# One kernel, three reorderings: a new opening, a first stage that projects one tile ahead, and a convolution stage with its gate products two tiles ahead

## The reference, cut to what matters

```python
h = rmsnorm(x, n1) * (1 + sc1) + sh1
u = h @ w_in                      # 1024 -> 7168 columns, split into branches
u_hy, u_fn, u_rx, u_ry, u_g = jnp.split(u, SPLITS, axis=-1)
kf  = hyena_filters(L, fw1, fb1, fw2, fb2, fw3, ffreq)   # two small sin layers, rfft
y_a = hyena_branch(u_hy, hcw, hcb, kf, hbias) @ w_a      # short conv, 2 long convs by FFT
y_b = fnet_branch(u_fn) @ w_b
xr  = depthwise_conv(u_rx, rcw, rcb, 2, 1)
h_f, s_f = rglru_scan(xr, ..., reverse=False); h_b, s_b = rglru_scan(xr, ..., reverse=True)
y_c = ((h_f + h_b) * gelu(u_ry)) @ w_c
ga, gb, gc = jnp.split(jax.nn.sigmoid(u_g), 3, axis=-1)
x = x + g1 * ((ga * y_a + gb * y_b + gc * y_c) @ w_o)    # then norm, SwiGLU FFN
```

## Time and profile before

| | before |
|---|---|
| median of three runs | 2571.53 us (2570.34 to 2575.14) |
| profiled execution | 2571.76 us, its span 2569.9 us |
| TensorE busy | 2479.5 us, 96% |
| DVE, ACT, GpSimd busy | 1460.8, 620.9, 696.0 us |
| mean granted clock of TensorE | 0.983 |
| DMA | 234.26 MB, mean 91 GB/s |

### The profile page before, as it was taken

The page is one execution under the profiler, slowest core; times in us unless marked ns, Lnnn a source line. Parts: engine busy times, 40 slices in busy tenths (PEclk is TensorE's granted clock), DMA queues, the critical chain, the costliest instruction groups (busy, mean ns, idle before and its releaser), DMA issues. The chain is left out here.

```text
span 2569.9 us, 34710 instructions
## 1 busy us (share of the span) xinstructions
PE 2479.5 (96%) x13478; PEld 2102.7 (82%) x13478; DVE 1460.8 (57%) x2697; ACT 620.9 (24%) x889; POOL 696.0 (27%) x300
## 2 busy tenths in 40 slices
PE   5799999999997999999999999999999999999997
PEld 2588888877876888888878878888888888888886
DVE  5878786678777676777763474633223322333236
ACT  4422222575753222222210012300000000000004
POOL 1011111223121222222333460442314331342220
PEclk8799999999998999999999999999999999999999
DMA  7244443111232222222453250111101010110002
GB/s 303 84 162 157 161 157 135 65 55 51 82 122 104 101 100 100 100 100 107 155 212 126 88 193 20 50 49 34 34 31 49 33 49 16 49 49 33 25 25 83
DMA packets 53755, 234.26 MB, mean 91 GB/s; under 512 B 6131, under 2 KB 8755, under 8 KB 48068
## 3 DMA queue, kind: packets, MB, share of 16 engines
q1 hardware_dynamic: 53700, 233.54, 25.2%
HBM read 178.98 MB, written 54.53 MB: 91 GB/s over the span
## 5 line engine op out<-in xcount | busy, mean ns | idle before, releaser
L840 PE MATMUL ps<-h_hi,w_hi 128*128 128x512 f32 (+1 forms) x2112 | 762.1, 361 | 13.5 <-DVE h_lo L1799 6.3
L841 PE MATMUL ps<-h_lo,w_hi 128*128 128x512 f32 (+1 forms) x2112 | 751.0, 356 | 0.0
L842 PE MATMUL ps<-h_hi,w_lo 128*128 128x512 f32 (+1 forms) x2112 | 750.9, 356 | 0.0
L798 POOL TENSOR_TENSOR w_hi<-w_raw,zero_col 128x1024 fp32r<-128x1024 f32 x96 | 206.4, 2150 | 1583.9 <-PE ps L842 1385.4
L840 PEld LDWEIGHTS ps<-h_hi,w_hi 128*128 128x128 f32 x2112 | 401.3, 190 | 78.8 <-issue 14.6
L842 PEld LDWEIGHTS ps<-h_hi,w_lo 128*128 128x128 f32 x2112 | 401.1, 190 | 57.1
L841 PEld LDWEIGHTS ps<-h_lo,w_hi 128*128 128x128 f32 x2112 | 401.5, 190 | 56.4 <-issue 0.2
L2151 DVE TENSOR_TENSOR a<-sil,ps 128x512 f32<-128x512 f32 (+1 forms) x66 | 39.5, 599 | 504.1 <-PE ps L842 501.7
L801 POOL TENSOR_TENSOR w_lo<-w_raw,w_hi 128x1024 fp32r<-128x1024 f32 x96 | 270.1, 2813 | 7.5
L2174 DVE SCALAR_TENSOR_TENSOR x<-ps,mod,x 128x512 f32<-128x512 f32 (+1 forms) x264 | 172.3, 661 | 98.1 <-PE ps L842 97.6
L841 PE MATMUL ps<-h_lo,wf_hi 128*128 128x512 f32 (+1 forms) x624 | 224.4, 360 | 0.0
(11 more groups left out here) (277 smaller groups left out, 3506.2 us busy)
## 6 DMA issues: line engine op xcount, KB each, us to landing
w_raw<-in_weights SPq DMA_DIRECT2D x146, 512.0 KB, 3.5
ada_w<-in_w_ada SPq DMA_DIRECT2D x18, 1024.0 KB, 8.1
scratch_gate_s<-g_st SPq DMA_DIRECT2D x24, 640.0 KB, 3.3
side<-scratch_gate_s SPq DMA_DIRECT2D x24, 640.0 KB, 4.0
scratch_k_s<-kstage SPq DMA_DIRECT2D x8, 1536.0 KB, 6.6
hy_k<-scratch_k_s SPq DMA_DIRECT2D x8, 1536.0 KB, 8.5
scratch_hy_s<-hout SPq DMA_DIRECT2D x16, 640.0 KB, 3.2
ada_early<-in_w_ada SPq DMA_DIRECT2D x6, 1024.0 KB, 22.2
```

The lines of the kernel that those rows point to most:

```text
L798: nc.gpsimd.tensor_tensor(hi[:], w_raw[slot % 2][:], zero_col[:].to_broadcast([P, D]), ALU.add).then_inc(pool_step, 1)
L840: mm(out, w_pair[0], x_pair[0], start=first, stop=False)
L841: mm(out, w_pair[0], x_pair[1], start=False, stop=False)
L842: return mm(out, w_pair[1], x_pair[0], start=False, stop=last)
```

## The change

**Opening.** The times of the filter network are laid out as two halves of 768, one in partitions 0 to 63 and one in 64 to 127 (`HALF_TILES`; the tiles 8 and 9 stand in both). `filter_layer` does each piece for both halves in separate quadrants of TensorE. ACT and DVE take 768 columns on 128 partitions in place of 1280. The squares come first, all of them summed before the first angle; the squares' product stands ahead of the second layer, the row product 0 before the broadcast of `rstd`. The four modulation rows have a row tile each; their turns go into one bank, and DVE adds the bias of all four in one instruction behind the scaling of x. `softplus` is moved behind the first stage.

**First stage.** Tile 1 is projected before the loop, and pass i holds tiles 2i+2 and 2i+3 where it held 2i+1 and 2i+2. The last pass holds tile 16, which belongs to the second stage, and the zeroing of the edges of `rin`. The first pair of the second stage is written out without tile 16, on TensorE and ACT. `load_ahead` of SyncE and its stores of `hout` are shifted in the same way.

**Convolution.** The first half is: tile t; transposes; tile t+1; tile t+2, piece 0; and goes on as the others. The others are: tile t, piece 2; tile t+1, pieces 0 and 1; transposes; tile t+1, piece 2; tile t+2, piece 0; forward transforms; tile t+2, piece 1; inverse singles and 2 pairs; tile t+2, piece 2; last 2 pairs; tile t+3, pieces 0 and 1, which the last half leaves out. ACT's gates and copies follow the same order, with tile t+2, piece 0 ahead of the `hy_z` copies. `store_gate` on SyncE, for the first gate of a half, stands ahead of the wait for `z_ready` and the loads. The store of the last scan and the states moves into the first half, behind its first gate store. The first channel block is written out; the loops run over the rest.

The core of the diff:

```diff
+HALF_TILES = ((0, 1, 4, 5, 8, 9), (2, 3, 6, 7, 8, 9))
+HALF_T = 6 * P
...
+            def filter_layer(layer, w_at, rows_at):
+
+                for j, (a, e) in enumerate(HALF_PIECES):
+                    out, done = mix_unit(u_setup, 0, FILT_UNIT[2 * layer + j])
+                    for half in range(2):
+                        rows = slice(half * FILT_HID, (half + 1) * FILT_HID)
+                        ins = mm(out[rows, 0:e - a], w_at(rows), rows_at(half, rows, a, e), start=True, stop=True)
+                    ins.then_inc(done, 1)
+
+            def row_product(r):
+                ada_row_unit(u_setup, 0, ROW_UNIT[r], [2 * r, 2 * r + 1], 16)
+
+            def row_turn(r):
+
+                if r == 0:
+                    mix_unit(u_setup, 0, TURN_UNIT)
+                pe.wait_ge(ada_row_ready, r + 1)
+                b = u_setup.bank(TURN_UNIT)
+                for q in range(4):
+                    ins = mm(mix(b)[:, 8 * r + 2 * q:8 * r + 2 * q + 2], ada_rows[r][:, q * P:(q + 1) * P],
+                             vec[:, V_SEL:V_SEL + 2], start=True, stop=True)
+                if r == ROWS_FIRST - 1:
+                    ins.then_inc(mix_done[b], 1)
...
             pe.wait_ge(consts_set, 3)
+            out, done = mix_unit(u_setup, 0, SQUARES_UNIT)
+            pe.wait_ge(x_sq_summed, KD - 1)
...
+            filter_layer(1, lambda rows: f_w2[rows, :], lambda half, rows, a, e: h1f[rows, a:e])
+
             pe.wait_ge(csilu_set, 2)
+            row_product(0)
+
+            pe.wait_ge(diag_ready, 1)
+            for b, (a, e, _) in enumerate(PIECES):
...
+            row_product(1)
+            row_product(2)
             pe.wait_ge(vec_in, 16)
...
+            row_turn(0)
+            row_turn(1)
+            row_product(3)
+            row_turn(2)
+            row_turn(3)
...
-                projection_tile(2 * i + 1, 1)
+                projection_tile(2 * i + 2, 0)
...
-                    projection_tile(2 * i + 2, 0)
+                    projection_tile(2 * i + 3, 1)
 
             projection_tile(0, 0, h_ready)
             taps_units(u_taps, 0, 0, 16)
+            projection_tile(1, 1)
...
+            def store_gate(c, j):
+                for b in range(3):
+                    sp.wait_ge(proj_free[b], 6 * c + (L3_TILE0 + j + 2))
+                sp.dma_start(dr["gate_s"][6 * c + j], g_st[:]).then_inc(gate_stored, 16)
...
                     load_ahead(t + 3 * order, 3 * order % 2)
-
+                    store_gate(c, 3 * order)
+                    if first and order == 0:
+                        sp.wait_ge(zc_ready, KD + 1)
+                        sp.wait_ge(zc_stored, 16 * KD + 16)
+                        sp.dma_start(dr["zc_s"][KD - 1], g_ry[1][:]).then_inc(zc_stored, 16)
+                        sp.dma_start(dr["state_out"], fin[:]).then_inc(fin_stored, 16)
+                        sp.wait_ge(zc_stored, 16 * (2 + KD))
                     sp.wait_ge(z_ready, 2 * c + (order + 1))
...
+            def l3_half(c, order, first, last):
...
+                if first:
+                    projection_tile(t, slot)
+                else:
+                    projection_tile(t, slot, pieces=(2,))
+                    projection_tile(t + 1, 1 - slot, pieces=(0, 1))
...
+                projection_tile(t + 1, 1 - slot, pieces=(0, 1, 2) if first else (2,))
+                projection_tile(t + 2, slot, pieces=(0,))
+
+                pe.wait_ge(hya_ready, 4 * c + (2 * order + 1))
...
+                projection_tile(t + 2, slot, pieces=(1,))
+
+                pe.wait_ge(y_ready, 4 * c + (2 * order + 1))
...
+                    if j == 2:
+                        projection_tile(t + 2, slot, pieces=(2,))
+                        pe.wait_ge(y_ready, 4 * c + (2 * order + 2))
...
+                if not last:
+                    projection_tile(t + 3, 1 - slot, pieces=(0, 1))
...
-                    gate(0)
+                    if first and order == 0:
+                        gate(0)
+                    else:
+                        gate(0, (2,))
+                        gate(1, (0, 1))
...
-                    gate(1, (0, 1))
+                    gate(1, (0, 1, 2) if first and order == 0 else (2,))
+                    gate(2, (0,))
```

More of the change, by code:

```diff
@@ L890, in _ @@
             pe.wait_ge(filt1_in, 32)
-            for j, (a, e, _) in enumerate(PIECES):
-                out, done = mix_unit(u_setup, 0, FILT_UNIT[j])
-                mm(out[0:FILT_HID, 0:e - a], f_w1[:, :], feats[:, a:e], start=True, stop=True).then_inc(done, 1)
+            filter_layer(0, lambda rows: f_w1[:, :], lambda half, rows, a, e: feats[:, half * HALF_T + a:half * HALF_T + e])
             pe.wait_ge(consts_set, 3)
+            out, done = mix_unit(u_setup, 0, SQUARES_UNIT)
+            pe.wait_ge(x_sq_summed, KD - 1)
@@ L896, in _ @@
+            for tile in range(NT):
+                ins = mm(out[:, 2 * tile:2 * tile + 2], x_sq_sum[:, tile * P:(tile + 1) * P], ones[:, 0:2],
+                         start=True, stop=True)
+            ins.then_inc(done, 1)
             pe.wait_ge(filt_in, 32)
             pe.wait_ge(sin_ready, 1)
-            for j, (a, e, _) in enumerate(PIECES):
-                out, done = mix_unit(u_setup, 0, FILT_UNIT[3 + j])
-                mm(out[:, 0:e - a], f_w2[:, :], h1f[:, a:e], start=True, stop=True).then_inc(done, 1)
+            filter_layer(1, lambda rows: f_w2[rows, :], lambda half, rows, a, e: h1f[rows, a:e])
@@ L1009, in fnet_tokens, with l2_pair @@
                     ins.then_inc(done, 1)
-            with pe.Fori(0, KD // 2) as m:
+            def l2_pair(m, first):
                 for s in range(2):
                     n = 2 * m + s
-                    projection_tile(2 * n + L2_TILE0, 0)
+                    if not (first and s == 0):
+                        projection_tile(2 * n + L2_TILE0, 0)
                     if s == 1:
@@ L1254, in take_filter @@
             def take_filter(layer):
-                rows = P if layer else FILT_HID
                 if layer:
@@ L1259, in take_filter, with take_row @@
                 act.wait_ge(f_bias_set, 1)
-                for j, (a, e, _) in enumerate(PIECES):
-                    src, free = take_mix(u_setup, 0, FILT_UNIT[3 * layer + j])
-                    fn(arg[0:rows, a:e], src[0:rows, 0:e - a], ACT.Identity, bias=f_bias[0:rows, layer:layer + 1],
-                       scale=f_vec[0:rows, 2:3]).then_inc(free, 1)
+                for j, (a, e) in enumerate(HALF_PIECES):
+                    src, free = take_mix(u_setup, 0, FILT_UNIT[2 * layer + j])
+                    fn(arg[:, a:e], src[:, 0:e - a], ACT.Identity, bias=f_bias[:, layer:layer + 1],
+                       scale=f_vec[:, 2:3]).then_inc(free, 1)
+            def take_row(r):
+                src, free = take_mix(u_setup, 0, ROW_UNIT[r])
+                own(fn(ada_rows[r][:, :], src[:, :], ACT.Copy))
+                act.sem_inc(free, 1)
+                act.sem_inc(ada_row_ready, 1)
             for k in range(KD):
@@ L1377, in l1_pass @@
                 own.restart()
+            conv_base(0, 0)
             taps_squares(0)
@@ L1501, in l3_pass @@
                             round_z(n)
-                    gate(2, (1, 2))
-            with act.Fori(0, CH - 1) as c:
-                l3_pass(c, False)
-            l3_pass(CH - 1, True)
+                    if not (last and order == 1):
+                        gate(3, (0, 1))
+            l3_pass(0, True, False)
+            with act.Fori(1, CH - 1) as c:
+                l3_pass(c, False, False)
+            l3_pass(CH - 1, False, True)
             for n in range(4, 16):
@@ L1679, in reduce_angle @@
             def reduce_angle(layer):
-                rows = P if layer else FILT_HID
-                for j in range(3):
-                    mix_taken(u_setup, 0, FILT_UNIT[3 * layer + j])
-                x, n = arg[0:rows, :], turns[0:rows, :]
+                for j in range(2):
+                    mix_taken(u_setup, 0, FILT_UNIT[2 * layer + j])
+                x, n = arg[:, :], turns[:, :]
                 own(ts(n, x, 1.0 / (2 * math.pi), ROUND, ALU.mult, ALU.add))
@@ L1873, in l1_pass @@
                 dve.sem_inc(fa_ready, 1)
-                conv_sides(2 * i + 1, 1)
+                if not last:
+                    conv_sides(2 * i + 2, 0)
+                else:
+                    zero_edges()
                 ada_add(units, it, 8, 2 * i + ADA_FIRST, 4)
@@ L1904, in _ @@
             l1_pass(7, u1_last, 0, True)
-            for a, e in ((0, PAD_LAT), (PAD_LAT + LAT, PAD_CTX), (PAD_CTX + CTX, PAD_T)):
-                own(nc.vector.memset(rin[:, a:e], 0.0))
-            dve.sem_inc(rin_zero, 1)
+            for part in range(3):
+                softplus(part)
             mix_taken(u1_last, 0, 4)
```

278 lines of the change are left out of this document (134 added, 144 removed).

## The result

| | before | after |
|---|---|---|
| median | 2570.94 us (2570.18 to 2575.14, 4 runs) | 2548.62 us (2545.34 to 2551.93, 4 runs) |
| profiled execution, its span | 2571.76, 2569.9 us | 2545.34, 2543.6 us |

The ratio is 0.9909, with a 95% interval of 0.9897 to 0.9922: 22.3 us less, where 17.5 were forecast. Terms are compared between the two profiles, the total between the medians; the profiles lie 4 us further apart than the medians.

What follows compares the result with a forecast made beforehand. TensorE was taken to bound the kernel almost everywhere, so gains come only where it waits or runs at half clock. 12 + 9.2 - 2 - 1.7 = 17.5 us off 2571.76 gave 2554 us, range 2540 to 2567.

Steps and rivals of the forecast that it cites:

- Opening, forecast 12: Start of the kernel: first projection at 52 instead of 63.94 us, a gain of 12 us (6 to 14.4).
- the column groups: Opening: 16 row products took 2.99 us in four column groups, so layer two's halves overlap and take 2.8 us.
- First pass, forecast 9.2: First stage: tile 1 fills a 15.0 us loss, a split collision leaves 5.8; gain 9.2 us (8 to 15).
- Border, forecast 2 lost: Change to the second stage: 0.9 us wait for xr, up to 1.4 from a split; cost 2 us (0 to 6).
- Convolution, forecast 1.7 lost: Long convolution: 10.6 + 3.1 - 7 - 8.4 = -1.7 us, ends -12 and +8.
- The first half: Convolution's first half: 19.3 us lost now, 8.7 lost after the edit, gain 10.6 us.
- The end: Convolution's last half: projection moved away turns into waits of 6.3 and 3.9 us; cost 8.4 us (6 to 11).
- The later halves: Convolution's seven other halves: gain 3.1 us in all, less 7 us for split collisions with DVE's even stage.
- DVE keeps the port: Rival for first stage and convolution: GpSimd waits instead of DVE; 2539 to 2547, say 2541 us; chance 0.27.
- the clock falls in each half: Rival in the convolution: seven waits each bring 6.8 us of half clock, 24 us lost, 2578 us; chance 0.07.
- ACT blocked in each half: Convolution rival: gate 1's store lands 2 us late seven times, 2568 us; chance 0.11, shared with a mixture near zero.
- The opening stays at half clock: Rival in the opening: first projection at 57.7 in place of 52, total 2560 us; chance 0.10.

Runs made afterwards that it cites:

- the first stage alone: Kernel before with only the first stage's edits, running one projection tile ahead: 2561.51 us, ratio 0.9967.
- early weights: Changed kernel with the weight loads of tiles 18 and 19 issued in the first stage's last pass, ahead of the spectrum's store: 2542.51 us, ratio 0.9897.
- where it was put inside: Changed kernel with two more DVE additions ahead of the first pass's even stage, so tile 2's split falls inside that stage: 2554.35 us, one run.
- The old place of the store: Changed kernel with each half's first gate store put back behind the wait for z and the loads: 2596.03 us, ratio 1.0097.
- the opening alone: Kernel before with only the opening's edits, softplus moved behind the first stage too: 2561.17 us, ratio 0.9963.

## Why the prediction held, and which of its terms did not

The total was right (22.3 measured, 17.5 forecast, within 2540 to 2567), and so was the sign. But two terms were wrong by 5 us in opposite directions, and one by 7. The four terms of the profiles sum to 24.2 us; that the medians came within 5 us of the forecast is in part luck.

**Opening, forecast 12, measured 11.5.** Layer two took 2.82 us for 1536 columns, as taken from the column groups. Two sizes ahead of it were off without effect, since `h1f` was ready only at 29.3: seven sums at 1.56 us from 12.5 end at 23.4 and not at 24.3 (they ended at 24.8), and the squares' product took 4.40 us, not 2.4. The place of the end was right for a wrong reason. TensorE's timeline of after, then two rows each of DVE and GpSimd:

```profile
24.94 4.40 PE L932 MATMUL ps<-ones,x_sq_sum 128*128 128x2 f32 x20 [13.84 <-DVE x_sq_sum L1751]
29.41 2.82 PE L907 MATMUL ps<-h1f,f_w 64*64 64x512 f32 x8
...
34.17 2.42 PE L945 MATMUL ps<-rstd_diag,ones 128*128 128x512 f32 x6
...
43.85 1.96 PE L920 MATMUL ps<-vec,ada_row 128*128 128x2 f32 x16
52.49 0.77 PE L851 MATMUL ps<-h_hi,w_hi 128*128 128x512 f32 x1 [6.68 <-DVE h_lo L1870]
...
47.19 1.94 DVE L1829 SCALAR_TENSOR_TENSOR norm_a<-mod,vec 128x8 f32<-128x8 f32 x2 [0.24 <-DVE mod L1821]
49.28 2.34 DVE L1856 TENSOR_SCALAR u_t<-x_in,norm_a,mod 128x512 f32<-128x512 f32 x1 [0.16 <-DVE norm_a L1829]
...
47.00 1.90 POOL L809 TENSOR_TENSOR w_hi<-w_raw,zero_col 128x1024 fp32r<-128x1024 f32 x1
48.97 2.36 POOL L812 TENSOR_TENSOR w_lo<-w_raw,w_hi 128x1024 fp32r<-128x1024 f32 x1
```

I made TensorE's queue of rows and turns the last thing, ending at 49.5, since I had the broadcast at half clock. The granted clock was 1.00 from 32.5 to 46.2 and 0.50 in the ten us after it, the turns ended at 45.8, and TensorE waited 6.68 us for `h_lo`. DVE was last: two scalings of 4.86 us from 36.59 to 46.5, bias, norms, and the first `h_lo` at 52.3. Turns placed 3.7 us too late and a chain behind them 3 us too short cancelled. The chain is longer by the same collision as elsewhere: the split of tile 1 meets it, and the norms take 1.94 us for the 0.37 of before, the first `u_t` 2.34 for 0.55, together 3.4. I had asked only whether the split holds TensorE, not what it costs DVE. The rows show the overlap in each profile of the new opening; no run was made without it. By all profiles the new opening starts its first projection at 52.3 to 53.6 us (ten) and the old one at 62.6 to 66.3 (four), 10.9 us apart in the mean.

**First pass, forecast 9.2, measured 14.2.** The step that failed is the timing, not the price. I had tile 1 done 19.1 us after tile 0, 1 us ahead of the end of DVE's stage. In after it was done after 20.2 us, because the taps products ran mostly at half clock (5.30 us for the 4.37 of before, granted clock 0.53), and DVE's stage ended after 20.2; in the kernel with the first stage alone it was done after 19.3, and the stage would have ended after 20.0 without the split. And of this second case, with tile 1 where I had it, only the last instruction was hit, at 0.48 us and no half clock in place of 3.4 and 2.4 us. A forecast that hangs on 1 us between two engines should have carried both outcomes with like weight. I gave the better one 0.27, and bound it to all the other collisions. They are separate cases: the first pass went one way and the border the other.

**Border, forecast 2 lost (0 to 6), measured 7.3, outside its own range.** The wait for `xr` was 0.48 us (forecast 0.9). What failed is the count of splits on the FNet stage: I moved one split there and priced it at 1.4 us. There are two. Before, tile 18's weights landed at 453 and were split beside `xr`; tile 19's split began when the stage was nearly over. With one tile less in front, the weights' landing (440.7, ten us after their issue behind `fn_t` and `fn_u`) and tile 17's end (437.7) came together at the start of the stage. At 3.8 us each they give the 7.7 that the stage was longer (439.47 to 451.2; before 460.25 to 464.3), 4.4 of it as a wait, and after it half clock (channel products 8.83 us for 7.07). The kernel with early weights shows it.

**Convolution, forecast 1.7 lost (-12 to +8), measured 5.6 won.** The first half gained 13.5 us, not 10.6 (from the transposes to the last inverse product 52.9 us in place of 58.0, with 8.4 more of projection in it): ACT was free at 799.7, 0.4 us from the place forecast (818.7 less the 18.6 won by then), but TensorE waited 2.74 in the transforms (3.5), 0.76 for `y_ready` (1.9), and the clock took 1.7 (2.6). The end lost 8.3 (forecast 8.4), by a wait of 6.5 us (6.3) and one of 2.0 (3.9). The later halves are the miss: 3.9 lost was forecast, 0.3 won. Only the even stage of two of seven was late, by 0.68. The same split, rows of GpSimd and DVE in one half that did not wait and in one that did:

```profile
851.23 3.49 POOL L809 TENSOR_TENSOR w_hi<-w_raw,zero_col 128x1024 fp32r<-128x1024 f32 x1 [10.45 <-PE ps L853]
...
852.75 2.05 DVE L229 TENSOR_SCALAR hy_a<-ztok 128x128 f32<-128x128 f32 x2
854.94 2.65 DVE L226 TENSOR_TENSOR hy_y<-ztok 128x384 f32<-128x384 f32 x1
...
911.62 2.99 POOL L809 TENSOR_TENSOR w_hi<-w_raw,zero_col 128x1024 fp32r<-128x1024 f32 x1 [4.66 <-PE ps L853]
...
912.78 1.98 DVE L223 TENSOR_TENSOR hy_a<-ztok 128x128 f32<-128x128 f32 x1
914.88 2.54 DVE L229 TENSOR_SCALAR hy_a<-ztok 128x128 f32<-128x128 f32 x2
...
917.60 1.60 PE L966 MATMUL ps<-hy_a,fwd 128*128 128x128 f32 x12 [0.68 <-DVEq L2082]
```

The full price is there in both, and in all seven: two instructions of DVE take 1.7 to 2.2 us more each. What differs is where they lie. In either half the even stage ends with the TENSOR_SCALAR pair. At 851.23 GpSimd's first instruction waited 1.6 us in DVE's stream, so only one hit fell into the even stage and the other (854.94) behind it, on work that TensorE needs later; the stage was in time. That is so in five of the seven. At 911.62 GpSimd waited 1.1, both hits fell inside, and TensorE waited. So the price per split was right, and what failed is that I put the whole of it into the even stage in all seven halves.

The Trainium skill ("SBUF — State Buffer", "Who interferes with whom") says that a `tensor_scalar` of DVE can enter a two-port mode and then contends with GpSimd as well. The rows at 111.39 and 98.92 agree: the second of the two one-input instructions of 128x128 took 1.92 us, where the first took 0.22.

**Rivals.** "DVE keeps the port" (2541) gave the number of the first pass but not its mechanism: the split came after the stage, and where it was put inside, DVE lost the 3.8 us. At the border and in the later halves DVE did not keep the port either; "the clock falls in each half" and "ACT blocked in each half" did not come: the granted clock was 1.00 in all of the seven later halves, behind the waits of 0.68 us too. The old place of the store shows what the latter would have been. "The opening stays at half clock" did not come.

## What to carry to other kernels

When work is moved ahead on the bounding engine, list where every helper's instructions that compete with another engine (here GpSimd's splits) will now start, and count them: each instruction of a split cost DVE 1.7 to 2.2 us inside a stage, and the split cost the stage nothing when it began a fifth of a microsecond after its end. Moving one load took it out (6 us at the border, 3 in the first half). Before work is pulled forward out of a loop's last pass, ask what it covered behind the loop's last result: here 8 us were worth giving back.

## What the runs showed of the hardware that was not expected

The same opening started its first projection at 62.6, 63.0, 63.9 and 66.3 us in the four profiles that have it unchanged; in the last one the row product and the squares behind it (33 to 41 us) took 3.64 and 4.43 us, 2.99 and 2.39 in before. The records of the granted clock show 1.00 from 33 to 43 us, so they do not explain it, and the cause stays open. So single profiles of this kernel differ by up to 4 us before any edit acts. In the kernel with the opening alone, where the two ACT functions of `softplus` have moved out of the opening, a table load of 1.28 us stands before an unrelated copy in every pass of a later loop, and TensorE waits 1.7 us for three of these copies. Before and after have none there; that the move brought it is read from the order of the program, and no run separates it from the rest of the opening's edits.
